# State-space outputs: three tables, outputs two blocks behind, the skip term in lag zero

## The reference

```python
y = uf * d_skip
for direction, reverse in ((0, False), (1, True)):
    a_bar = jnp.exp(a * dt)
    bu = jnp.einsum('blgp,gnp->blgn', ug, b_bar)
    _, states = lax.associative_scan(_linear_combine, (a_seq, bu), axis=1, reverse=reverse)
    y = y + jnp.einsum('blgn,gpn->blgp', states, c).real.reshape(bsz, l, S5_WIDTH)
```

## Time and profile before

| what | value |
|---|---|
| time, median of 3 runs | 3356.51 us (3352.04 to 3356.57) |
| the profiled execution | 3353.25 us, span 3351.5 us |
| PE busy | 2669.1 us, 80% |
| DVE busy | 1410.2 us, 42% |
| ACT busy | 963.2 us, 29% |
| POOL busy | 978.3 us, 29% |
| mean granted clock of PE | 0.902 |

### The profile page before, as it was taken

One profiled execution on the slowest core, in us unless ns is written; L12 is line 12 of the kernel. 1 busy time (PEld: TensorE's weight loads), 2 busy tenths in 40 slices (PEclk: granted clock), 3 DMA queues, 4 the chain that ended last, 5 costly groups with the idle time before them and its releaser, 6 DMA issues. The chain is left out here.

```text
span 3351.5 us, 46224 instructions
## 1 busy us (share of the span) xinstructions
PE 2669.1 (80%) x15442; PEld 2277.5 (68%) x15442; DVE 1410.2 (42%) x2424; ACT 963.2 (29%) x1698; POOL 978.3 (29%) x1156
## 2 busy tenths in 40 slices
PE   3979997469988645579868999979999936666698
PEld 3858886458888544567647888848999924544477
DVE  4433335336766655232243444540110147766414
ACT  3212221563333333412322222231000024544331
POOL 1323331027775000331204433404354401111310
PEclk9989998679999777789988999989999968988799
DMA  5212223301010133444323242453243343332344
GB/s 111 72 45 93 94 78 72 30 26 39 19 38 19 34 62 63 127 137 145 121 93 112 98 154 87 148 182 100 88 133 126 99 176 128 125 145 102 112 153 169
DMA packets 267221, 331.43 MB, mean 99 GB/s; under 512 B 43088, under 2 KB 215018, under 8 KB 265842
## 3 DMA queue, kind: packets, MB, share of 16 engines
q1 hardware_dynamic: 222514, 217.92, 22.3%
q10 hardware_dynamic: 44608, 112.34, 9.2%
HBM read 213.94 MB, written 112.07 MB: 97 GB/s over the span
## 5 line engine op out<-in xcount | busy, mean ns | idle before, releaser
L279 POOL TENSOR_TENSOR w_hi<-w_raw,ones 128x512 fp32r<-128x512 f32 (+1 forms) x248 | 266.4, 1074 | 1373.4 <-PE r L292 679.6
L280 POOL TENSOR_TENSOR w_lo<-w_raw,w_hi 128x512 fp32r<-128x512 f32 (+1 forms) x248 | 323.7, 1305 | 19.4
L292 PE MATMUL r<-h_lo,w_hi 128*128 128x264 f32 (+1 forms) x1344 | 305.8, 336 | 18.1 <-POOL w_lo L280 18.1
L292 PE MATMUL r<-h_hi,w_hi 128*128 128x264 f32 (+1 forms) x1344 | 288.3, 323 | 0.0
L292 PE MATMUL r<-h_hi,w_lo 128*128 128x264 f32 (+1 forms) x1344 | 286.4, 321 | 0.0
L292 PEld LDWEIGHTS r<-h_lo,w_hi 128*128 128x128 f32 x1344 | 200.3, 190 | 45.1 <-POOL w_lo L280 18.7
L292 PEld LDWEIGHTS r<-h_hi,w_lo 128*128 128x128 f32 x1344 | 195.0, 189 | 20.6
L292 PEld LDWEIGHTS r<-h_hi,w_hi 128*128 128x128 f32 x1344 | 194.4, 189 | 19.3
L292 PE MATMUL r<-xc_lo,w_hi 128*128 128x264 f32 (+2 forms) x864 | 186.2, 324 | 5.6 <-ACT fx L2123 5.6
L292 PE MATMUL r<-xc_hi,w_hi 128*128 128x264 f32 (+2 forms) x864 | 185.5, 323 | 0.0
L292 PE MATMUL r<-xc_hi,w_lo 128*128 128x264 f32 (+2 forms) x864 | 183.9, 321 | 0.0
(11 more groups left out here) (346 smaller groups left out, 5556.2 us busy)
## 6 DMA issues: line engine op xcount, KB each, us to landing
w_raw<-in_w_in_even SPq DMA_DIRECT2D x72, 256.0 KB, 3.2
w_raw<-in_w_in_odd SPq DMA_DIRECT2D x64, 256.0 KB, 3.3
w_raw<-in_w_ogate SPq DMA_DIRECT2D x64, 256.0 KB, 5.0
v_d<-vs ACTq DMA_DIRECT2D x8, 1152.0 KB, 5.7
v<-v_d SPq DMA_DIRECT2D x8, 1152.0 KB
xc_d<-sg ACTq DMA_DIRECT2D x8, 1040.0 KB, 4.4
z_d<-zs ACTq DMA_DIRECT2D x8, 1040.0 KB, 6.5
xz_d<-xz ACTq DMA_DIRECT2D x8, 1040.0 KB, 6.5
```

The costliest lines, as they stand in the source:

```text
L279: do(self.nc.gpsimd.tensor_tensor(hi, raw, one, ALU.mult))
L280: self.nc.gpsimd.tensor_tensor(lo, raw, hi.bitcast(F32), ALU.subtract).then_inc(self.split.sem, 1)
L292: ins = self.nc.tensor.matmul(region[:, PO + off:PO + off + n], w[:, b, k, :], z[:, off:off + n], start=(first and k == 0 and w is self.hi ...
```

## The change

`s5_outputs` now works with three buffers of `tab` (block modulo 3), two each of `kt` and `ys`, and four PSUM tiles `yp`. `ys` lies in `vt`, the memory of the attention's v, which is free by then. The skip term is no longer added to `toe`: DVE builds once, for all groups, a tile `diag` of 16x1024 (skip times identity) and adds it to the 16x16 block of lag zero as it copies it into `kt`. The windows then bring it to the diagonal. DVE has no turn that waits for `toe`, only tables(n), lags(n) for each n. PE does lags(n+1) and then mix(n-1), not mix(n). ACT gathers two blocks ahead, behind the stores: outputs of n, stores of n, gather(n+2). SP loads the `us` of block n when mix(n-2) is done, then its windows when `kt` of n is complete. The hardware loops are gone: all eight blocks are straight-line code. The core of the diff:

```diff
-        table = s.sb("tab", [P, 2, 2, GB, T, GP])
+        diag = s.sb("diag", [GP, G, GP])
+        table = s.sb("tab", [P, 3, 2, GB, T, GP])
         tmp = s.sb("tmp", [P, 2, GB // 2, T, GP])
-        kt = s.sb("kt", [GP, GB, K])
+        kt = s.sb("kt", [GP, 2, GB, K])
         toe = s.sb("toe", [P, 2, GB, P])
         rhs = s.sb("rhs", [P, 2, GB, 2, CH])
-        ys = s.sb("ys", [P, GB, CH])
+        ys = vt[:, :, :].rearrange("p t f -> p (t f)")[:, 0:2 * GB * CH].rearrange("p (b g c) -> p b g c", b=2, g=GB)
         ends = [s.ps(f"lags{b}", 512) for b in range(2)]
         zero = [s.ps(f"lag_zero{b}", 512) for b in range(2)]
-        yp = [s.ps(f"yp{b}", 512) for b in range(3)]
-        u_loaded = [s.flag(f"u_loaded{b}", per=8 * T) for b in range(2)]
-        built = s.flag("table_built", per=2)
-        gathered = s.flag("states_gathered", per=2)
-        lag = s.flag("lags_done", per=2, credit=2)
-        lagc = s.flag("lags_copied", per=2, credit=2)
-        windowed = s.flag("windows_loaded", per=16 * T, credit=16)
-        toe_ready = s.flag("toeplitz_ready", per=1)
-        done = s.flag("outputs_done", per=GB, credit=2 * GB)
-        ycop = s.flag("outputs_copied", per=GB, credit=GB)
-        ysto = s.flag("outputs_stored", per=16 * T, credit=16)
+        yp = [s.ps(f"yp{b}", 512) for b in range(4)]
...
+                def load_u(n):
+                    if n >= 2:
+                        sp.wait_ge(done, (n - 1) * GB)
                     for j in range(T):
-                        sp.dma_start(us[j * GP:(j + 1) * GP, b, :, :],
-                                     uv[j][:, bass.ds(n * GB, GB), :]).then_inc(u_loaded[b].sem, 16)
-                def load(n, b, more):
-                    lagc.wait(sp, n, 2)
+                        sp.dma_start(us[j * GP:(j + 1) * GP, n % 2, :, :],
+                                     uv[j][:, n * GB:(n + 1) * GB, :]).then_inc(u_loaded[n % 2], 16)
+                def windows(n):
+                    sp.wait_ge(lag_copied, 2 * n + 2)
...
+                load_u(0)
+                load_u(1)
+                windows(0)
+                windows(1)
+                for n in range(2, NB):
+                    load_u(n)
+                    windows(n)
...
+                do.free(v.memset(apart[:, :, :, :], 0.0))
+                do(v.tensor_tensor(diag[:, :, :], t["skip"][0:GP, :].unsqueeze(2).broadcast_to([GP, G, GP]),
+                                   c["ident"][0:GP, 0:GP].unsqueeze(1).broadcast_to([GP, G, GP]), ALU.mult))
+                def tables(n):
...
+                        if n >= 3:
+                            dve.wait_ge(done, (n - 3) * GB + HALF * (m + 1))
...
+                def lags(n):
                     for m in range(2):
-                        lag.wait(dve, n, m + 1)
-                        if m == 0:
-                            windowed.wait(dve, n, 0)
-                        dst = kt[:, m * HALF:(m + 1) * HALF, :]
+                        dve.wait_ge(lag, 2 * n + m + 1)
+                        if n >= 2 and m == 0:
+                            dve.wait_ge(windowed[n % 2], 16 * T * (n // 2))
+                        dst = kt[:, n % 2, m * HALF:(m + 1) * HALF, :]
...
-                def turn(n, b, more):
-                    windowed.wait(dve, n, 16 * T)
-                    for m in range(GB):
-                        ins = v.scalar_tensor_tensor(toe[:, b, m, :], c["ident"][:, :],
-                                                     t["skip"][:, bass.ds(n * GB + m, 1)],
-                                                     toe[:, b, m, :], ALU.mult, ALU.add)
-                        do(ins) if m == GB - 1 else do.free(ins)
-                    dve.sem_inc(toe_ready.sem, 1)
-                    if more:
...
+                        v.tensor_tensor(dst[:, :, BACK:BACK + GP],
+                                        zero[m][0:GP, 0:HALF * GP].rearrange("p (g k) -> p g k", g=HALF),
+                                        diag[:, n * GB + m * HALF:n * GB + (m + 1) * HALF, :], ALU.add)
+                        v.tensor_copy(dst[:, :, BACK + GP:K], src[0:GP, :, 0:BACK]).then_inc(lag_copied, 1)
+                for n in range(NB):
+                    tables(n)
+                    lags(n)
...
+                def mix(n):
+                    b = n % 2
+                    pe.wait_ge(u_loaded[b], 16 * T * (n // 2 + 1))
+                    pe.wait_ge(gathered, 2 * n + 2)
+                    pe.wait_ge(windowed[b], 16 * T * (n // 2 + 1))
                     for m in range(GB):
-                        ycop.wait(pe, n, max(m - 2, 0))
-                        o = yp[m % 3][:, 0:CH]
+                        at = n * GB + m
+                        if at >= 4:
+                            pe.wait_ge(y_copied, at - 3)
...
+                lags(0)
+                for n in range(NB):
+                    if n + 1 < NB:
+                        lags(n + 1)
+                    if n:
+                        mix(n - 1)
+                mix(NB - 1)
...
+                def gather(n):
+                    if n >= 2:
+                        act.wait_ge(done, (n - 1) * GB)
...
+                def evict(n):
+                    b = n % 2
+                    if n >= 2:
+                        act.wait_ge(y_stored[b], 16 * T * (n // 2))
                     for m in range(GB):
-                        done.wait(act, n, m + 1)
-                        nc.scalar.activation(ys[:, m, :], yp[m % 3][:, 0:CH], ACT.Copy).then_inc(ycop.sem, 1)
-                    ycop.wait(act, n, GB)
+                        at = n * GB + m
+                        act.wait_ge(done, at + 1)
+                        nc.scalar.activation(ys[:, b, m, :], yp[at % 4][:, 0:CH], ACT.Copy).then_inc(y_copied, 1)
...
+                gather(0)
+                gather(1)
+                for n in range(NB):
+                    evict(n)
+                    if n + 2 < NB:
+                        gather(n + 2)
```

More of the change, by code:

```diff
@@ L1105, in s5_outputs @@
     HALF = GB // 2
+    NB = G // GB
     with stage(nc) as s:
@@ L1133, in s5_outputs @@
         yv = d["y"].rearrange("g p s c -> s p g c")
[L1134 to L1142, removed]
         with nc.Block() as block:
@@ L1168, in _ @@
                 do = Steps(dve, steps)
-                lagc.start(dve)
-                windowed.start(dve)
                 f, r = slice(0, NS), slice(NS, P)
-                do(v.memset(apart[:, :, :, :], 0.0))
-                def tables(n, b):
-                    g = bass.ds(n * GB, GB)
-                    lag.wait(dve, n, 0)
+                do.free(v.memset(apart[:, :, :, :], 0.0))
+                do(v.tensor_tensor(diag[:, :, :], t["skip"][0:GP, :].unsqueeze(2).broadcast_to([GP, G, GP]),
+                                   c["ident"][0:GP, 0:GP].unsqueeze(1).broadcast_to([GP, G, GP]), ALU.mult))
+                def tables(n):
+                    g = slice(n * GB, (n + 1) * GB)
+                    if n:
+                        dve.wait_ge(lag, 2 * n)
                     do.free(v.tensor_copy(bb[:, :, :, :], t["B"][:, :, g, :]))
@@ L1183, in tables @@
                     for m in range(2):
-                        done.wait(dve, n, -2 * GB + HALF * (m + 1))
-                        half = bass.ds(n * GB + m * HALF, HALF)
-                        do(complex_table(nc, do, table[:, b, :, m * HALF:(m + 1) * HALF], tmp,
+                        if n >= 3:
+                            dve.wait_ge(done, (n - 3) * GB + HALF * (m + 1))
+                        half = slice(n * GB + m * HALF, n * GB + (m + 1) * HALF)
+                        do(complex_table(nc, do, table[:, n % 3, :, m * HALF:(m + 1) * HALF], tmp,
@@ L1221, in _, with lags @@
+                for n in range(NB):
+                    tables(n)
+                    lags(n)
             @block.tensor
             def _(pe):
-                lag.start(pe)
-                done.start(pe)
                 flat = "p t q -> p (t q)"
-                def lags(n, b):
+                def lags(n):
                     for m in range(GB):
@@ L1230, in lags @@
                         if at == 0:
-                            built.wait(pe, n, h + 1)
-                            lagc.wait(pe, n, h - 1)
+                            pe.wait_ge(built, 2 * n + h + 1)
+                            if n:
+                                pe.wait_ge(lag_copied, 2 * n - 1 + h)
                         for q in range(2):
@@ L1240, in lags @@
                             last = nc.tensor.matmul(ends[h][0:32 + GP, at * P:(at + 1) * P], apart[:, q, m, :],
-                                                    table[:, b, q, m].rearrange(flat),
+                                                    table[:, n % 3, q, m].rearrange(flat),
                                                     start=(q == 0), stop=(q == 1))
                         if at == HALF - 1:
-                            last.then_inc(lag.sem, 1)
-                def turn(n, b, more):
-                    if more:
```

(25 more changed lines are left out.)

54 lines of the change are left out of this document (22 added, 32 removed).

## The result

The changed kernel takes **3297.29 us** (median of 4 runs, 3294.29 to 3302.17); the kernel before took 3356.54 beside it (4 runs, 3352.04 to 3360.65). The ratio is 0.9824, with a 95% interval of 0.9811 to 0.9836: 59 us or 1.8% faster. The forecast was 3308 in a range of 3290 to 3326. The sign and the range held; the gain was 59 us and not 48. So the agreement with that rival is a coincidence of sizes.

The account below looks back on a forecast made before the run. A ring of waits through the windows' DMA bound the output stage at 26.5 us a block; with ACT's 16.7 us rounds next, 55.4 us gained less 9.2 for the clock gave 46.2, so 3307.0, put at 3308 us (3290 to 3326).

Parts of the forecast that it names:

- that rival: Rival "the clock holds": PE's stalls at the output tiles do not bring the clock down; 3298 us, chance 0.27.
- The ring: Output stage: skip, tables, lags, copies of kt and windows' landing wait on each other in turn, 26.5 us a block.
- What is late next: ACT's copies, stores and gather in the output stage set the round at 16.7 us, over 15.5 of DVE and PE.
- The stores' issue: Term in ACT's round: 5.26 us from the stores' first issue to the gather.
- the case: Rival on ACT's queue: stores' issue gets cheap, 3.72 us and not 5.05, DVE and PE bind; 3289 us, chance 0.10.
- The clock: Term for PE's stalls inside mixes: four of six bring half clock at 2.3 us each, 9.2 us off the gain.
- Last copy of mix(0): Start of ACT's last copy for block 0, put at 1180.6 after two rounds of 15.5; mix(0) delayed 6.0 us.
- The forecast's lags piece: Eight groups of lags on PE, with DVE's copies beside them: 8.6 us of the 15.5 us DVE and PE round.
- The last mix: Mix(7), with no gather ahead of it: 0.44 + 5.26 + 3.26 = 9.0 us after mix(6)'s last copy.
- The clock rivals: Two rivals on PE's clock: it holds, 3298 us, chance 0.27; it is down nearly throughout, 3326 us, chance 0.12.
- the 3.1 a round of the rival: Rival "clock down nearly throughout": PE binds at 19.8 us a round, six rounds 3.1 longer each; 3326 us, chance 0.12.
- slower: Rival: straight-line code stops an engine for lack of code, up to 17.9 us per block pair; 3361 us, chance 0.03.

Follow-up runs that it names:

- the two fastest orders: Changed kernel with one block of distance and stores on SP, 3273.23 us; that kernel with the copies of B and C on GpSimd, 3262.88 us.

## Why the prediction was right, and where its size was off

**What held.** The ring and what leaves it: the skip and the windows' round trip were what the stage waited for, and taking out that part alone gave the whole gain and more. What is late next is ACT, in the order copies, stores, gather, with PE standing in front of the fifth group. Nothing waited for windows, `rhs` or the second `kt`. Straight-line code, the end of the stage and the rest of the program cost nothing, as forecast.

**The terms of the sum**, each with what it measured. From stage start (the first gather, 1128.10 before and 1129.79 after) to last copy, the forecast puts 1301.5 on the clock of before and the trace 1285.1 (1286.79 less the 1.69 by which the stage began later): 16.4 us too long.

- The stores' issue, taken as 5.26 us a round up to the gather from the earlier trace rows, was 3.8 to 4.2 in every round (3.7 to 3.9 for the issue itself): 1.35 x 7 = 9.4 us. **This is the term that was most mis-sized.** The prediction named the case as a rival, gave it 0.10, and argued against it that SP's loads run beside the stores and that beside such loads the stores took 5.14. Loads alone do not do it: the changed kernel issues the same loads beside the stores in six rounds, and they take 3.8 to 3.9; with windows beside them, 7.0 to 7.9. What the prediction passed over stands in its own rows: the windows of the earlier trace rows were issued until 1175.80, and the stores of the earlier trace rows began at 1174.99. In all seven dear rounds of the kernel before, the stores began 0.5 to 1.4 us before the windows' issue ended; the eighth (3.72) had neither windows nor loads beside it. So the windows are the likely cause there. It is not proved: no run takes them alone out of the kernel before, and two rounds of the kernel with one block of distance had dear stores (4.69 and 5.25 us) without them. The Trainium skill (DMA: Bandwidth & Descriptors, Issuing engines are not separate DMA queues) says that DMAs of different engines interleave on the same 16 DMA engines and that the issue time is usually small relative to the DMA. The first is in line with one queue stretching the other. The second holds for one store (0.46 us of issue, 2.9 to landing, the medians of the changed kernel). The prediction set it against the issue of eight, which is another comparison. It is the sum of the eight that counts: a quarter of ACT's round (3.86 of 15.35), and taking it off ACT shortened the stage by 11 us.
- The clock: forecast four falls at 2.3 us and 2.3 more for mix(6), 11.5 in all. Measured four in the six rounds, mix(6)'s among them: 98.9 us of rounds, 6.5 over six of 15.4. That is 5.0 less. The number of falls was nearly right, by luck as much as by reason: the stalls were 0.6 to 2.2 us and not 3 to 5, because the stores were cheap. Each fall slowed two or three groups and not four, since the clock was back 3.5 us later.
- Last copy of mix(0): forecast 1180.6, measured 1178.8 (1180.47 less 1.69), 1.8 less. `kt` of block 0 was complete 0.5 sooner than forecast; `diag` took 1.15 us and not 1.4. The two rounds of DVE and PE before mix(0), 15.5 each in the forecast, took 14.32 and 15.37 (copies of `B` at 1146.52, 1160.84 and 1176.21), 1.3 less. The forecast's lags piece was read where five of eight groups ran at half clock, 1.24 us apart as in the earlier trace rows. Three groups did so in the first of these two rounds, which cost nothing, and five in the second, which cost about 1 us; a later round with none took 14.44 (1190.64 to 1205.08).
- The last mix: 9.0 forecast, 7.44 measured; the stores, counted above, are all but 0.2 of it.

Together 9.4 + 5.0 + 1.8 + 0.2 = 16.4. The forecast is 10.7 us and not 16.4 over the measured median because its errors elsewhere go the other way: the stage began 1.7 us later, what follows it took 2 us more, and the median lies 3.0 above the profiled execution where 1 was allowed.

**The clock rivals.** The clock neither held nor stayed down. The Trainium skill (TensorE: Matmul & The Clock Gate, A second HAM failure mode: psum-queue depth-cycling) describes such a swing; this trace has it, at 1.5 us in four of six rounds and not at the 3.1 a round of the rival. Before the last two blocks three of its falls came in such stalls. With the stalls gone (stores on SP) one fall was left there, among the lags, and none once the copies were on GpSimd.

**The price of "slower"** rests on a misread row. The 17.9 us of the earlier trace rows stand before weight loads (PEld), and PE's own row for that line is `PE r L2064 <- DMA buffer<-xc_d: 24.9, 8, 17.6`: a DMA is named for that idle time. It is no bound on what missing code could cost. The run with straight-line code alone settles the rival.

**What the prediction did not ask** is what each part of the change is worth by itself. It had the two numbers for it: the windows hidden "with 11 us to spare", and mix(0) 6.0 us later, "paid once". Against the kernel before that delay measured 4.2 us of start (41.75 from first gather to first copy, 1128.10 to 1169.85, and now 46.0). Against the kernel that has the skip in lag zero and keeps the distance of one block it is 14.8, because there the start shrinks to 31.2. For that the depth and the buffers gave back 6.0: 1.6 in six rounds and 4.3 in the last block.

## What to carry to other kernels

When a ring of waits runs through a DMA round trip, take the round trip out of the in-order engine's program (here by folding the term in ahead of the transfer) before adding buffers. Depth beyond what hides the transfer delayed the first result by 14.8 us here and won back 6. DMA issue is work on its engine's queue. If that engine sets the round, move the issue to an idle queue, and look at what other transfers run beside it: the same eight stores cost 3.8 or 7 to 7.9 us by the order of two lines on another engine. With fewer blocks of distance look at the last block too: its windows came 4 to 8 us late in the two fastest orders.

## What the runs showed of the hardware

- Issue of eight stores on ACT's queue: 3.7 to 3.9 us alone or beside loads of `us` in the changed kernel, 5.1 to 5.8 where they began while windows were being issued, 7.0 to 7.9 fully beside them. The windows' own issue went from 5.3 to 6.4 us in the changed kernel to 7.1 to 8.0. But 4.69 and 5.25 were also seen beside loads alone (one block of distance), and 5.62 on SP's queue with nothing on ACT's, 2.31 of it a single store (stores on SP). What stretches those is not shown.
- A silence of PE of 2.2 us was followed by half clock, one of 1.8 was not. But at 1142.5 the clock stayed up through 3.5 us, and the groups behind silences of 3.12 us (the skip term alone, at 1184.8) and 2.44 us (one block of distance, at 1174.9) ran at full clock. So the length of one silence does not decide it alone.
- GpSimd needs 1.2 us for a 64x256 copy that DVE does in 0.28, and 0.40 for the 128x256 one (DVE 0.27). Of DVE's 128x512 operations beside such copies one took 0.67 us and two 0.78 and 0.87; elsewhere they took 0.67 to 0.69.
